# An attention and MLP layer: q, k and v projected twelve tiles ahead in place of sixteen, weights split in a head's fourth step

## The reference

```python
u = rms_norm(x, norm1_g)
q, k, v = split(u @ w_in, 3)              # 8 heads; q and k: two parts of 64 each, v: 128
q, k = rms_norm(q, q_g), rms_norm(k, k_g)
s = q @ k.T * 64 ** -0.5                  # for each of the two parts, causal in chunks of 64 rows
p = softmax(s); pd = p[part 0] - lam * p[part 1]
o = rms_norm(pd @ v, sub_g) * (1 - lambda_init)
h = x + o @ w_out
h = h + square(relu(rms_norm(h, norm2_g) @ w1)) @ w2
```

## Time and profile before

| what | value |
|---|---|
| median of 3 runs (lowest to highest) | 2808.23 us (2804.86 to 2811.44) |
| the profiled execution's own time, and its span | 2805.49 us, 2803.7 us |
| busy: TensorE, VectorE, ScalarE, GpSimd | 97%, 68%, 54%, 38% of the span |
| granted TensorE clock, mean | 0.993 |
| projections (L421), all | 3072 matmuls, 934 us busy |
| attention of head 0 begins; the last head begins | 111.5 us; 1226.6 us |
| GpSimd: w_lo (L400); w_out_lo (L733) | 26 of 1.83 us; 8 of 2.36 us |

### The profile page before, as it was taken

How to read it: one execution, slowest core, us unless ns; L and a number is a source line. 1 busy time by engine, 2 the same in 40 slices (tenths; PEclk the granted TensorE clock), 3 DMA queues, 4 the chain that set the end, 5 groups by cost and what they waited for, 6 DMA issues and landing times.

```text
span 2803.7 us, 42849 instructions
## 1 busy us (share of the span) xinstructions
PE 2721.1 (97%) x14784; PEld 2369.1 (84%) x14784; DVE 1896.4 (68%) x2726; ACT 1501.0 (54%) x2987; POOL 1076.4 (38%) x956
## 2 busy tenths in 40 slices
PE   7999999999999999979999999999999999999999
PEld 7898989989898999967887788888888888888887
DVE  6777787777778787775776666656555555666655
ACT  5666666666666666664554444444444444344443
POOL 5633424243433424331000354444343444444443
PEclk9999999999999999989999999999999999999999
DMA  8742424243242423223455996666667976666663
GB/s 267 263 142 86 161 97 153 94 150 113 94 153 86 161 97 128 98 86 142 155 183 188 353 371 239 236 235 251 269 247 277 364 280 237 233 232 239 235 236 130
DMA packets 181808, 544.09 MB, mean 194 GB/s; under 512 B 14736, under 2 KB 88208, under 8 KB 136592
## 3 DMA queue, kind: packets, MB, share of 16 engines
q1 hardware_dynamic: 180016, 541.25, 52.7%
q10 hardware_dynamic: 1632, 0.79, 0.1%
HBM read 470.81 MB, written 71.17 MB: 193 GB/s over the span
## 4 chain that ended last, share of the span: by engine, by line
PE 83%; issue 6%; DVE 4%; ACT 3%; DMA 2%; POOL 1%; SPq 0%; ACTq 0%; POOLq 0%; DVEq 0%
PE banks L2163 21%; PE banks L2139 21%; PE banks L421 17%; PE banks L666 5%; PE banks L563 4%; PE banks L565 4%; PE banks L638 4%; PE banks L825 3%; PE banks L668 2%; PE banks L513 2%; ACT pt_hi L647 1%; DMA u<-u_factors 1%; ACT p_all L605 1%; DVE mx L582 1%; DVE p_all L627 1%
## 5 line engine op out<-in xcount | busy, mean ns | idle before, releaser
L2139 PE MATMUL banks<-u,w 128*128 128x512 f32 x2688 | 614.6, 390 | 3.8 <-issue 2.0
L421 PE MATMUL banks<-w_hi,u_ring 128*128 128x384 f32 x2048 | 589.1, 347 | 10.8 <-DVE u_ring L1315 4.2
L2139 PEld LDWEIGHTS banks<-u,w 128*128 128x128 f32 x2688 | 505.5, 188 | 109.9 <-issue 3.8
L2163 PE MATMUL banks<-w,a_hi 128*128 128x512 f32 x1792 | 552.1, 389 | 1.5 <-issue 1.0
L1905 POOL TENSOR_TENSOR w<-w_raw,w 128x1024 fp32r<-128x1024 f32 x96 | 245.2, 2568 | 553.5 <-ACT w L1954 278.5
L605 ACT ACTIVATE p_all<-banks,bias 128x1024 f32<-128x1024 f32 (+7 forms) x384 | 331.7, 866 | 182.5 <-DVE bias L585 116.0
L2163 PEld LDWEIGHTS banks<-w,a_hi 128*128 128x128 f32 x1792 | 336.3, 188 | 72.3 <-issue 2.3
L421 PEld LDWEIGHTS banks<-w_hi,u_ring 128*128 128x128 f32 x2048 | 375.9, 188 | 15.6 <-issue 9.7
L2163 PE MATMUL banks<-w,a_lo 128*128 128x512 f32 x896 | 348.8, 389 | 0.0
L451 POOL TENSOR_TENSOR qk_rs<-qk_var,minus_half 128x4 f32<-128x4 f32 x128 | 129.4, 1011 | 563.4 <-DVE qk_var L445 563.4
L421 PE MATMUL banks<-w_lo,u_ring 128*128 128x384 f32 x1024 | 344.6, 337 | 0.0
(11 more groups left out here) (151 smaller groups left out, 4724.3 us busy)
## 6 DMA issues: line engine op xcount, KB each, us to landing
u<-u_factors SPq DMA_DIRECT2D x224, 1024.0 KB, 9.4
u_ring<-u_scratch SPq DMA_DIRECT2D x112, 1024.0 KB, 5.2
w_raw<-in_mlp_w SPq DMA_DIRECT2D x128, 512.0 KB, 6.7
u_scratch<-u_ring SPq DMA_DIRECT2D x16, 1024.0 KB, 5.0
u_factors<-q_hi SPq DMA_DIRECT2D x23, 512.0 KB, 4.4
u_factors<-q_lo SPq DMA_DIRECT2D x23, 512.0 KB, 4.3
w_raw<-in_a_w_in SPq DMA_DIRECT2D x90, 128.0 KB, 4.6
p_all<-in_x SPq DMA_DIRECT2D x16, 512.0 KB, 5.7
```

What stands on the lines that cost most here:

```text
L421: last = pe.matmul(proj[:, 0:3 * HD], u[:, part, kt, :], w[:, kt, :], start=(kt == 0 and part == 0 and w is w_hi), stop=(kt == KT - 1 and ...
L2139: last = pe.matmul(banks[:, UP_BANKS[p] + f, :], w[:, 2 * k2 + k, f * P:(f + 1) * P], u[:, :, part, k, :], start=(STARTS[p] and k2 == 0 an ...
L2163: last = pe.matmul(banks[:, DOWN_BANKS[p] + t, :], a[:, p % 2, f, t * P:(t + 1) * P], b[:, f, :], start=(STARTS[p] and f == 0 and a is a_h ...
```

## The change

Tile n's projection is placed in step n - 12 (`LEAD`). The ramp has twelve steps; all sixteen u's are turned in it, two in its fourth and seventh step and the last behind it (`TURNED_WITH`), and u's 12 to 15 are projected out of the ring in the first four attention steps, ahead of the scores in the very first. A head's weights are needed from j = 4 of the head before, so they are split in j = 3 (`SPLIT_AT`) in all seven cases: GpSimd's low part of piece 0 ahead of its work on q and k, piece 2 behind it, piece 3 behind the output's factor, VectorE's piece 1 behind its combine. In the last head j = 0 to 3 project tiles 124 to 127; the output weights are split two by two in j = 1 to 4, each pair once the u that lay in its place has been projected, and the first product waits for them one by one. The raw weights are loaded from j = 6, not j = 4.

```diff
@@ -33 +33 @@
+LEAD = 12
+SPLIT_AT = NT - LEAD - 1
+TURNED_WITH = ((1,), (2,), (3,), (4, 5), (6,), (7,), (8, 9), (10,), (11,), (12,), (13,), (14,), (15,))
@@ high_w_out @@
-        if kt == 0:
-            act.wait_ge(proj_half, 2 * ALL)
+        act.wait_ge(proj_half, 2 * (ALL - US + kt // 2 + 1))
@@ load_o, load_x @@
-            sp.wait_ge(proj_half, 2 * ALL)
             sp.dma_start(g2_row[:, :], norm2_g.to_broadcast([P, D])).then_inc(g2_loaded, 16)
...
     def load_x(sp, t):
+        if t == 0:
+            sp.wait_ge(proj_half, 2 * ALL)
@@ pe_product @@
-                pe.wait_ge(w_out_lo_set, KT)
...
             for kt in range(part * HALF, part * HALF + HALF):
+                if t == 0 and d == 0:
+                    pe.wait_ge(w_out_lo_set, kt + 1)
@@ sync @@
-            if a + NT + 3 < ALL:
-                load_u(sp, a + NT + 3)
-            if j == 4 and h + 2 < H:
+            if NT <= a + LEAD + 3 < ALL:
+                load_u(sp, a + LEAD + 3)
+            if j == SPLIT_AT + 3 and h + 2 < H:
                 load_weights(sp, h + 2, range(4))
@@ gpsimd, small_step @@
+            splits = j == SPLIT_AT and h + 1 < H
+            if h == H - 1 and j == US:
+                low_w_out(pool, KT - 2)
+                low_w_out(pool, KT - 1)
+            if splits:
+                low_weights(pool, h + 1, 0)
             if n < ALL:
                 pool_factor_qk(pool, n)
                 pool_norm_qk(pool, n)
                 low_v(pool, n)
+            if splits:
+                low_weights(pool, h + 1, 2)
             if j:
                 pool_output(pool, a - 1)
-            if h == H - 1 and j <= 3:
-                low_w_out(pool, 2 * j)
-                low_w_out(pool, 2 * j + 1)
+            if splits:
+                low_weights(pool, h + 1, 3)
+            if h == H - 1 and 1 <= j < US:
+                low_w_out(pool, 2 * j - 2)
+                low_w_out(pool, 2 * j - 1)
@@ gpsimd, big_step @@
-            if j == NT - 1 and h + 2 < H:
-                low_weights(pool, h + 2, 0)
-                low_weights(pool, h + 2, 1)
...
-            if j == NT - 1 and h + 2 < H:
-                low_weights(pool, h + 2, 2)
-                low_weights(pool, h + 2, 3)
@@ scalar, small_step @@
             for g in range(1, nb):
                 act_turned_p(act, a - 1, g)
+            if h == H - 1 and j == US:
+                high_w_out(act, KT - 2)
+                high_w_out(act, KT - 1)
             if t >= 1:
                 act_turned_u2(act, t - 1)
+            if j == SPLIT_AT and h + 1 < H:
+                act_split_weights(act, h + 1, (0, 1))
...
             if a:
                 act_output_low(act, a - 1)
                 act_square_output(act, a - 1)
-            if h == H - 1 and 1 <= j <= 3:
-                high_w_out(act, 2 * j)
-                high_w_out(act, 2 * j + 1)
+            if j == SPLIT_AT and h + 1 < H:
+                act_split_weights(act, h + 1, (2, 3))
+            if h == H - 1 and 1 <= j < US:
+                high_w_out(act, 2 * j - 2)
+                high_w_out(act, 2 * j - 1)
@@ scalar, big_step @@
-            if j == NT - 1 and h + 2 < H:
-                act_split_weights(act, h + 2, (0, 1))
...
-            if j == NT - 1 and h + 2 < H:
-                act_split_weights(act, h + 2, (2, 3))
@@ vector, small_step @@
+            if j == SPLIT_AT and h + 1 < H:
+                low_weights(dve, h + 1, 1)
             if n < ALL:
                 dve_sum_qk(dve, n)
@@ tensor @@
-        for j in range(NT):
-            if j + 1 < NT:
-                turn_u(j + 1)
+        for j in range(LEAD):
+            for t in TURNED_WITH[j]:
+                turn_u(t)
             pe_project(pe, j, 0)
             pe_project(pe, j, 1)
             if j:
                 pe_turn_qk(pe, j - 1)
+        turn_u(NT - 1)
@@ tensor, small_step @@
+            if a == 0:
+                pe_project(pe, n, 0)
+                pe_project(pe, n, 1)
             pe_scores(pe, a, 0)
             pe_scores(pe, a, 1)
@@ on every engine @@
-                big_step(a, a + NT, nb)
+                big_step(a, a + LEAD, nb)
```

More of the change, by code:

```diff
@@ L142, in turn_order @@
 def turn_order():
-    order = [("qk", n) for n in range(NT - 1)]
+    order = [("qk", n) for n in range(LEAD - 1)]
     for a in range(H * NT):
         h, j = split(a)
-        qk = [("qk", a + NT - 1)] if a + NT - 1 < H * NT else []
+        qk = [("qk", a + LEAD - 1)] if a + LEAD - 1 < H * NT else []
         p = [("p", a - 1, n) for n in range(banks_of((a - 1) % NT))] if a else []
@@ L1003, in sync @@
         store_u(NT - 2)
-        load_u(sp, NT)
         store_u(NT - 1)
-        for n in range(NT + 1, NT + 3):
-            load_u(sp, n)
         for a in range(ALL):
             h, j = split(a)
-            if a + NT + 3 < ALL:
-                load_u(sp, a + NT + 3)
-            if j == 4 and h + 2 < H:
+            if NT <= a + LEAD + 3 < ALL:
+                load_u(sp, a + LEAD + 3)
+            if j == SPLIT_AT + 3 and h + 2 < H:
                 load_weights(sp, h + 2, range(4))
@@ L1087, in gpsimd @@
         x_factor(2)
-        for j in range(NT):
-            if j == NT - 1:
-                low_weights(pool, 1, 0)
+        for j in range(LEAD):
             pool_factor_qk(pool, j)
-            if j + 3 < NT:
-                x_factor(j + 3)
+            for t in TURNED_WITH[j + 1]:
+                if t + 1 < NT:
+                    x_factor(t + 1)
             pool_norm_qk(pool, j)
@@ L1130, in gpsimd @@
         for a in range(ALL):
-            (big_step if a % NT >= BIG else small_step)(a, a + NT)
+            (big_step if a % NT >= BIG else small_step)(a, a + LEAD)
         pool_output(pool, ALL - 2)
@@ L1164, in scalar @@
         act.wait_ge(eps_set, 1)
-        for j in range(NT):
-            if j + 2 < NT:
-                x_square(j + 2)
-            if j + 1 < NT:
-                high_u(j + 1)
+        for j in range(LEAD):
+            for t in TURNED_WITH[j]:
+                if t + 1 < NT:
+                    x_square(t + 1)
+                high_u(t)
             if j == 0:
@@ L1180, in scalar @@
                 act_turned_qk(act, j - 1)
-        act_split_weights(act, 1, (2, 3))
+        high_u(NT - 1)
         def first_step(a, n, nb):
@@ L1277, in scalar @@
             if a % NT >= BIG:
-                big_step(a, a + NT, nb)
+                big_step(a, a + LEAD, nb)
             elif a and a % NT == 0:
-                first_step(a, a + NT, nb)
+                first_step(a, a + LEAD, nb)
             else:
-                small_step(a, a + NT, nb)
+                small_step(a, a + LEAD, nb)
         act_output_low(act, ALL - 2)
@@ L1346, in vector @@
         dve.memset(mask_r[0:1, :], MASKED).then_inc(consts_set, 1)
-        for j in range(NT):
-            if j + 2 < NT:
-                u_norm(j + 2)
-            if j + 1 < NT:
-                low_u(j + 1)
+        for j in range(LEAD):
+            for t in TURNED_WITH[j]:
+                if t + 1 < NT:
+                    u_norm(t + 1)
+                low_u(t)
             if j == 0:
                 lambdas_and_gains()
-            if j == NT - 1:
-                low_weights(dve, 1, 1)
             dve_sum_qk(dve, j)
@@ L1358, in vector @@
                 dve_turned_qk(dve, j - 1)
-        low_weights(dve, 1, 2)
-        low_weights(dve, 1, 3)
+        low_u(NT - 1)
         dve.wait_ge(lam_step, 4)
@@ L1377, in small_step @@
         def small_step(a, n, nb):
-            t = output_tile(*split(a))
+            h, j = split(a)
+            t = output_tile(h, j)
             dve_max(dve, a, 0, 0)
@@ L1515, in small_step @@
                 pe_turn_p(pe, a - 1, 0)
-            if n < ALL:
+            if a and n < ALL:
                 pe_project(pe, n, 0)
```

5 lines of the change are left out of this document (removed).

## The result

| | before | after |
|---|---|---|
| median, device us | 2807.09 (6 runs, 2804.86 to 2811.44) | 2860.84 (6 runs, 2855.01 to 2863.22) |
| ratio, 95% interval | | 1.0183 [1.0172, 1.0194] |
| span of the profiled execution | 2803.7 us | 2858.7 us |
| granted clock, mean | 0.993 | 0.987 |

The change costs 53.8 us; 2854 was forecast, with a range of 2826 to 2876. In the changed kernel `w_lo` is written at L403 (before L400), `w_hi` at L399 (L396), the projection's matmuls are L424 (L421), the combine is L630 (L627), `w_out_lo` L735 (L733), the output product L829 (L825), norm and low part of u are L1312 and L1317 (L1310, L1315).

What follows compares the result with a forecast made beforehand. TensorE, busy for 97% of the span, was taken as the bound. Terms -9.9 - 2.6 + 42.7 + 9.8 + 5.8 = +45.8 on the profiled 2805.49 us gave 2851.3; with 2.7 to the median, 2854, range 2826 to 2876.

Steps and rivals of the forecast that it cites:

- ramp, with its switch of weights: Ramp: four projections leave, -9.9 us; the split of head 1's weights at its end goes, -2.6.
- seven switches: idle time: Weight splits in the fourth step of heads 0 to 6: TensorE loses 6.1 us each, +42.7 in all.
- seven switches: the rest, mostly clock: After each switch's stall the clock drops to its lower level: 1.4 us each, +9.8 in all.
- last head: Last head: projections join GpSimd's loop of output-weight pairs, so the first product ends later, +5.8 us.
- near 106: Sign at the ramp's end: the first scores start near 106, the last u turned near 101.6.
- rival (c): Ramp: TensorE sets the pace after all, -19.7 us in place of -9.9, total 2844; chance 0.08.
- whatever TensorE does: Ramp: the loop of low part, x load, square and norm takes 5.9 us a tile, independent of TensorE.
- The chain of instructions: Fourth step of head 3: low parts and q, k work queue up from 620.92 until low part 3 at 629.2.
- (a): Rival at the seven switches: they stay hidden as before the change, total 2801.5; chance 0.08.
- (b): Rival at the seven switches: partly hidden, 2.6 us each as in the ramp, total 2820; chance 0.08.
- Rival (d): Seven switches: the clock falls for twice as long at each, +9.8 us more, total 2864; chance 0.12.
- 0 to 9: Bounds on the last head's +5.8 us; 0 if the projections only fill idle time.

Runs made afterwards that it cites:

- e3: Changed kernel with one store of u less ahead of each load of x on SyncE's queue in the ramp: 2859.48 us, ratio 1.0179.
- e4: Kernel before the change, with one store of u less ahead of each load of x on SyncE's queue: 2805.47 us, ratio 0.9989.
- e6: Changed kernel; VectorE makes all four low parts of a switch in a row, ScalarE's late high parts come before squaring q and k: 2816.59 us, 1.0032.
- e5: Changed kernel; VectorE makes all four low parts of a switch, two behind its combine, two at the step's end: 2826.56 us, 1.0068.
- e1: Changed kernel without loads and splits of later heads' weights; head 0's serve all heads (result partly wrong): 2801.81 us, 0.9974.
- e7: Changed kernel; a head's first projection runs sixteen high-part matmuls, then turns q and k and does values, then eight low-part matmuls: 2832.70 us, 1.0084.
- e2: Changed kernel with the output weights' low parts in the last head on VectorE in place of GpSimd: 2852.36 us, ratio 1.0155.
- e13: e12 with one store of u less ahead of each load of x in the ramp: 2813.76 us, ratio 1.0018.
- e10: Changed kernel with e7's order, e3's queue, early high parts, all low parts on VectorE, a switch's parts 2 and 3 one step later: 2832.96 us, 1.0082.
- e12: Changed kernel with e6's split and e2's edit, plus p's high and low parts ahead of exps and maxes after the split: 2817.31 us, 1.0027.

## Why the prediction was right, point by point

| term | forecast | measured |
|---|---|---|
| ramp, with its switch of weights | -9.9 - 2.6 = -12.5 | -11.2 |
| seven switches: idle time | +42.7 | +38.4 |
| seven switches: the rest, mostly clock | +9.8 | +17.3 |
| clock in other steps | 0 | +2.9 |
| last head | +5.8 | +7.4 |
| sum | +45.8 | +54.8 |

The mechanism was right in the main, and the time lies 7 us above the forecast. That it is so near is partly luck: inside the switches the idle time was put 4.3 us too high and its second price 7.5 too low.

**The ramp.** The sum held: first scores at 106.2 ("near 106"). The reason was only half right. The last low part of a u is begun at 103.44 (before at 103.01), so the loop did keep its pace, and rival (c), TensorE alone, is out: by it 22.3 us would have gone with the ramp's switch, and 11.2 did. In the other kernels with this ramp the first scores start up to 2.3 us later, so the term is good to about 2 us. But "whatever TensorE does" was too much said: in the kernel before TensorE was busy for 97% of that stretch, and e3 and e4 show that an earlier load gives some 2 to 3.5 us of the first scores' start, not 5 to 10. Nor did the sum have a term for the clock, which fell at both steps that turn two u's.

**The switch.** The chain of instructions came as laid out. It was forecast at 8.3 us from TensorE's first want to low part 3 (620.92 to 629.2); from 633.28 to 640.99 it took 7.7. TensorE was idle for 5.48 us in place of 6.1, in each of the seven. What was left out is that each stop costs more than its idle time: e6 has one stop of 1.46 and is 1.82 longer than 7.35, e5 has two of 2.70 together and is 3.30 longer, both at the full clock, so 0.3 to 0.36 a stop. In the changed kernel 15.23 less 7.35 is 7.88: 5.48 idle, 0.6 for two stops by that (an estimate), and the rest, 1.8, the clock, which was forecast at 1.4 from a product's matmuls. By the same reckoning the clock took 1.3 to 2.7 us in the seven heads, 1.9 on average. e1 shows that the 55.7 are the switches'; e5 that the time follows the last low part; e7 that it follows TensorE's want for it. Rivals (a), hidden, and (b), 2.6 each, are out: the least of the seven costs 7.4. Rival (d), the clock down for twice as long, would make a switch 8.9, and it was in part right. The mean clock of the step was 0.88 or 0.89 in heads 0, 1 and 6 (7.4 to 7.5 us over 7.35) and 0.78 or 0.79 in heads 2 to 5, so that it was down for about twice as long there. Heads 2, 4 and 5 lost 8.3 to 8.75 us; head 3 lost 7.9, since part of its lower clock fell into the idle time.

The clock was down behind every one of the seven stalls. That agrees with the rule of the Trainium skill ("TensorE: Matmul & The Clock Gate", "Why this matters for your kernels") that idle gaps between bursts of matmuls cost rate; but not every gap does: with gaps of 2.30 us the clock stayed at 1.00 in six of e5's seven switches, with gaps of 1.81 us in four of e7's.

**The clock elsewhere.** The sum had no term for the first steps of heads 4 and 5. No row of before pointed to it, and the runs don't say what brings it: kernels whose first steps have the same order show it in two heads (the changed kernel, e2), in one (e5, e13) or in none (e3, e6).

**The last head.** Pairs of output weights were forecast to end 15.4, 24.4, 33.5 and 40.2 us after the second step's start; they ended 15.4, 24.2, 33.2 and 39.6 (from 1289.58), the first product's matmuls at 40.6 (40.9). In the kernel before the first product ended 35.1 after, so this part is +5.5. The step that fell short is that the sum stopped at the first product. The second one, begun at 1330.98 with the clock partly at its lower level, took 7.37 us where 5.75 is its full pace, 1.6 more, and what stands behind it in the step took 1.1 more. The head's first step was 0.7 shorter and the later ones 0.1 together. That makes the +7.4. The bracket "0 to 9" held it. e2 shows the cause: with the pairs on VectorE the head is 6.1 us shorter. In kernels whose last head is the same the fifth step takes 23.4 to 25.7 us (e1, e5, e6, e7, e3), with another mean clock in each, so this term is good to a microsecond or so.

## What to carry to other kernels

What a moved step costs is read where it lands: work that was free behind a step of 13.7 us cost 8 us behind one of 7.35, and the reckoning that found it was a list of who is next on each in-order queue, with durations from the trace, up to the time at which the bottleneck engine wants the result. When such a chain is too long, first look who is slow in it (two low parts on VectorE cost as much as one on GpSimd, and started beside each other the second only waits for the first), then whether the consumer can do another part first, and stop when the chain's next member starts to shift: here two further orders (e10, e12) only moved the wait on. A stop of the bottleneck engine should be priced with what it costs beyond its idle time (0.3 to 0.36 us here) and with the clock that may follow.

## What the runs showed of the hardware

The granted clock does not follow from the idle time of a step alone. In the changed kernel the first step of a head has 2.3 us of idle TensorE in heads 1 to 7 (15.28 long and 13.02 busy in head 3; 16.83 and 14.58 in head 4), and yet the clock is 1.00 in one and 0.90 in the other, for 1.55 us. In e10 six of those seven first steps were so; in the kernel before none of heads 1 to 6, with 2.4 idle. Likewise e10's switches have 2.52 to 2.53 us of idle time each: the clock is 0.86 in six of them and 1.00 in head 4's. What tips it stays open. What a fall cost ranges from 0.6 us (a switch of e7, 11.09 against 10.47) over 1.5 to 1.6 (first steps, e10's switches) to some 2.7 (head 2's switch in the changed kernel, by the reckoning above).

A VectorE instruction with two SBUF operands and one of GpSimd's do not share: the one that starts second waits for the first. GpSimd's low part in head 3 starts at 630.72, while VectorE's combine (630.45, 0.75 long) runs, and takes 2.19 us in place of 1.80. VectorE's low part starts at 631.40 and takes 2.32 in place of the 0.89 that it takes by itself (four in 3.56); it ends at 633.72, 0.81 after GpSimd's, which ended at 632.91. In the earlier trace rows GpSimd's starts first, with no combine before it, and keeps its 1.83; VectorE's, begun 0.55 later, takes 2.09 and ends 0.81 after it. So the pair is slower than VectorE alone doing both, and only the second to start pays.
